# The last level of a block inverse in 32x32 products instead of 64x64 ones, in a transformer kernel on one Trainium2 core

## What is computed

```python
def step(state, inp):
    r_t, w_t, k_t, v_t, kk_t, a_t = inp
    sa = jnp.einsum('bhij,bhj->bhi', state, -kk_t)
    state = (state * w_t[:, :, None, :] + sa[..., None] * (kk_t * a_t)[:, :, None, :]
             + v_t[..., None] * k_t[:, :, None, :])
    return state, jnp.einsum('bhij,bhj->bhi', state, r_t)
```

## Time and profile before

| What | us |
|---|---|
| Median of three runs | 1789.96 |
| Lowest, highest | 1787.77, 1790.02 |
| The profiled execution's own time | 1789.94 |
| Its span in the trace | 1788.6 |
| TensorE busy in the span | 1765.4 |
| VectorE, ScalarE, GpSimd busy | 1155.0, 945.4, 128.3 |

### The profile page before, as it was taken

The page is one execution under the profiler, slowest core; times in us unless marked ns, Lnnn a source line. Parts: engine busy times, 40 slices in busy tenths (PEclk is TensorE's granted clock), DMA queues, the critical chain, the costliest instruction groups (busy, mean ns, idle before and its releaser), DMA issues.

```text
span 1788.6 us, 26360 instructions
## 1 busy us (share of the span) xinstructions
PE 1765.4 (99%) x10762; PEld 1476.6 (83%) x10762; DVE 1155.0 (65%) x1589; ACT 945.4 (53%) x1433; POOL 128.3 (7%) x90
## 2 busy tenths in 40 slices
PE   9999999999999999999999999999999999999999
PEld 6888888888888888888888878888888888888887
DVE  5555678676555565556786755555697557697556
ACT  6454675345544454447653554444646554656553
POOL 0100010141000000000002210000002000002000
PEclk9999999999999999999999999999999999999999
DMA  8755542134555557555421436555554455554564
GB/s 285 279 190 186 173 152 85 61 105 130 187 185 186 186 187 253 186 169 188 142 84 61 140 116 223 189 188 170 165 180 156 166 193 193 174 177 153 174 190 130
DMA packets 84343, 301.12 MB, mean 168 GB/s; under 512 B 9728, under 2 KB 10880, under 8 KB 83712
## 3 DMA queue, kind: packets, MB, share of 16 engines
q1 hardware_dynamic: 80192, 289.44, 49.1%
q10 hardware_dynamic: 3712, 8.56, 1.4%
q0 software_dynamic: 320, 1.45, 0.3%
HBM read 298.36 MB, written 1.05 MB: 167 GB/s over the span
## 4 chain that ended last, share of the span: by engine, by line
PE 88%; DVE 6%; ACT 4%; issue 1%; DMA 1%; POOL 0%; SPq 0%; DVEq 0%; ACTq 0%
PE ps L400 25%; PE ps L402 25%; PE ps L401 25%; DVE wlo L380 1%; ACT whi L339 1%; PE ps L623 1%; PE ps L1278 1%; PE ps L1266 1%; DMA raw<-stream 1%; DVE a_lo L476 1%; PE ps L2680 1%; PE ps L809 1%; PE ps L460 1%; PE ps L423 1%; PE ps L421 1%
## 5 line engine op out<-in xcount | busy, mean ns | idle before, releaser
L380 DVE TENSOR_TENSOR wlo<-raw,whi 128x1024 fp32r<-128x1024 f32 (+1 forms) x545 | 668.9, 1236 | 360.1 <-ACT whi L339 358.6
L339 ACT ACTIVATE whi<-raw 128x1024 fp32r<-128x1024 f32 (+1 forms) x545 | 570.7, 1053 | 454.2 <-PE ps L402 423.7
L400 PE MATMUL ps<-whi,a_hi 128*128 128x512 f32 x1712 | 677.2, 396 | 5.9 <-DVE a_lo L2013 2.0
L402 PE MATMUL ps<-whi,a_lo 128*128 128x512 f32 x1712 | 664.7, 388 | 0.0
L401 PE MATMUL ps<-wlo,a_hi 128*128 128x512 f32 x1712 | 663.7, 388 | 0.0
L400 PEld LDWEIGHTS ps<-whi,a_hi 128*128 128x128 f32 x1712 | 321.5, 188 | 74.5 <-issue 4.7
L402 PEld LDWEIGHTS ps<-whi,a_lo 128*128 128x128 f32 x1712 | 321.3, 188 | 67.6
L401 PEld LDWEIGHTS ps<-wlo,a_hi 128*128 128x128 f32 x1712 | 321.9, 188 | 61.6
L400 PE MATMUL ps<-whi,h_hi 128*128 128x512 f32 x336 | 131.6, 392 | 0.0
L402 PE MATMUL ps<-whi,h_lo 128*128 128x512 f32 x336 | 130.9, 390 | 0.0
L401 PE MATMUL ps<-wlo,h_hi 128*128 128x512 f32 x336 | 130.8, 389 | 0.0
(11 more groups left out here) (330 smaller groups left out, 1680.6 us busy)
## 6 DMA issues: line engine op xcount, KB each, us to landing
raw<-stream SPq DMA_DIRECT2D x545, 512.0 KB, 3.4
arena<-rows ACTq DMA_DIRECT2D x2, 1026.0 KB, 13.8
arena<-mem_turned ACTq DMA_DIRECT2D x2, 1024.0 KB, 9.1
arena<-lora ACTq DMA_DIRECT2D x2, 768.0 KB, 6.6
arena<-x_turned SPq DMA_DIRECT2D x4, 256.0 KB, 6.4
x_res<-x SPq DMA_DIRECT2D x2, 512.0 KB, 9.4
arena<-mem ACTq DMA_DIRECT2D x1, 1024.0 KB, 12.2
arena<-rows ACTq DMA_DIRECT2D x2, 512.0 KB, 4.6
```

Source lines behind the costliest of these rows:

```text
L339: self.split_hi.mark(act.activation(self.weights(self.whi, u), self.weights(self.raw, u), ACT.Copy), u)
L380: self.split_lo.mark(dve.tensor_tensor(self.weights(self.wlo, u), self.weights(self.raw, u), self.weights(self.whi, u).bitcast(F32), ALU.s ...
L400: pe.matmul(out, a_h, hi, start=start, stop=False, skip_group_check=True)
L402: last = pe.matmul(out, a_l, hi, start=False, stop=True, skip_group_check=True)
```

## The change

The last level gets a function of its own, `pe_rw_last_level`, that `pe_mix` calls in place of `pe_rw_level(l, 5)`. It has the same waits, marks and number of products. Each product now loads 32 rows x 32 columns and streams 32 columns: the first half computes only the rows 32 to 63 and columns 0 to 31 of the product in between (rows `down`, columns `first`), from the matrix's rows `up` and columns `last`. The second computes only the block of rows `up` and columns `last`, from the rows `down`. The rest of each bank keeps what was there, which the mask doesn't let through. ScalarE and VectorE are unchanged, and so is the order of all engines.

```diff
@@ pe_rw_level
             for h in range(8):
                 for c in range(2):
                     co = slice(c * HD, (c + 1) * HD)
-                    pair = (T[co, 0, h, :], X[co, h, :]) if lv < 5 else (X[co, h, :], T[co, 0, h, :])
-                    ins = pe.matmul(self.x8(t)[co, h, :], *pair, start=True, stop=True, skip_group_check=True)
+                    ins = pe.matmul(self.x8(t)[co, h, :], T[co, 0, h, :], X[co, h, :], start=True, stop=True,
+                                    skip_group_check=True)
+            m.mark(ins, "level", l, t, lv)
+
+    def pe_rw_last_level(self, l):
+
+        pe, m, lv = self.nc.tensor, self.rw_pe, 5
+        first, last = slice(0, HD // 2), slice(HD // 2, HD)
+        rows = [(slice(c * HD, c * HD + HD // 2), slice(c * HD + HD // 2, (c + 1) * HD)) for c in range(2)]
+        for t in range(NT):
+            pe.wait_ge(*self.rw_dve("T", l, t, lv - 1))
+            for h in range(8):
+                for up, down in rows:
+                    ins = pe.matmul(self.x8(t)[down, h, first], self.MK[up, t, 2 * (h % 4) + h // 4, 0, last],
+                                    self.T2[t][up, 1, h, first], start=True, stop=True, skip_group_check=True)
+            m.mark(ins, "level x", l, t, lv)
+        for t in range(NT):
+            pe.wait_ge(*self.rw_act("X", l, t, lv))
+            pe.wait_ge(*self.rw_dve("turned", l, t, lv - 1))
+            for h in range(8):
+                for up, down in rows:
+                    ins = pe.matmul(self.x8(t)[up, h, last], self.XG[t][down, h, first], self.T2[t][down, 0, h, last],
+                                    start=True, stop=True, skip_group_check=True)
             m.mark(ins, "level", l, t, lv)
@@ pe_mix
         self.pe_rw_gate(l, 0, 2)
-        self.pe_rw_level(l, 5)
+        self.pe_rw_last_level(l)
         pe.wait_ge(*self.rw_act("bonus", l))
         self.pe_rw_gate(l, 1, 3)
```

More of the change, by code:

```diff
@@ L1264, in pe_rw_level @@
                 for c in range(2):
-                    co = slice(c * HD, (c + 1) * HD)
-                    ins = pe.matmul(self.x8(t)[co, h, :], self.MK[co, t, 2 * (h % 4) + h // 4, 0, :], self.T2[t][co, 1, h, :],
-                                    start=True, stop=True, skip_group_check=True)
+                    co, n = slice(c * HD, (c + 1) * HD), 2 * (h % 4) + h // 4
+                    ins = pe.matmul(self.x8(t)[co, h, :], self.MK[co, t, n, 0, :], self.T2[t][co, 1, h, :], start=True,
+                                    stop=True, skip_group_check=True)
             m.mark(ins, "level x", l, t, lv)
```

## The result

| | Runs | Lowest | Median | Highest | Mean granted clock of a run |
|---|---|---|---|---|---|
| Before | 19 | 1786.22 | 1787.77 | 1791.12 | not recorded |
| With the change | 19 | 1787.32 | 1793.07 | 1794.52 | 0.992 to 0.997 |

The change makes the kernel slower: the ratio is 1.0017, 95% interval 1.001 to 1.0024, some 3 us. The medians lie 5.3 us apart: both kernels' runs stand in clusters, and the middle run falls into different ones. The forecast was 1786.6 us with a range from 1783.9 to 1790.1. It was wrong.

A forecast was written before the change was run, and what follows sets the result against it. TensorE, busy for 99% of the span, was taken as the bound. Savings of 1.4 us in layer 1 and 1.9 us in layer 0 made 3.3 us off 1789.94, giving 1786.6 us, range 1783.9 to 1790.1.

The forecast's parts named there:

- What bounds the kernel: Whole kernel: TensorE, busy 99% of the span; time off its row counts unless the next wait gives it back.
- Pace: Last level's products: a pair of records takes 30 ns instead of 58, in proportion to the columns loaded.
- both floors: Last level's record pace: L1214's 27 to 30 ns a record, and the skill's about 25 ns between starts.
- The level at the full clock: Last level in layer 1: 2.5 us in place of 3.9, 1.4 us less, with ScalarE's copies as its bound.
- The lower clock lasts until 339.8, if it lasts as long as before: Last level and gate in layer 0: the low clock ends at the same time as before, giving 1.9 us less.
- The clock falls once more: Rival, behind L1424: a further 6.9 us stretch at half clock costs up to 3.45 us, giving 1790.1; chance 0.12.
- thin products keep the clock low: Rival, last level: 32-column products double layer 0's low stretch and bring two in layer 1, 1797.0 us; chance 0.06.
- The clock falls less often: Rival, last level: no fall in the median execution, 2.5 us in both layers, giving 1784.0 us; chance 0.20.

The follow-up runs named there:

- e6: The kernel before, with its eight two-column products issued four between level 4's halves and four behind it: 1786.53 us, ratio 0.9992.
- e10: e8 with the second gate's first product moved between the halves of the last level: 1783.53 us, ratio 0.9969 to the kernel before.
- e2: The change, but streaming 64 columns instead of 32, still on 32 rows with 32 columns loaded: 1793.27 us, ratio 1.0021 to the kernel before.
- e7: The change, with the eight two-column products issued four and four as in e6: 1790.97 us, ratio 1.0012 to the kernel before.
- e9: The change run once more, with no edit: 1789.47 us, ratio 1.0016 to the kernel before.
- e5: The change, but loading 64 columns instead of 32, still on 32 rows with 32 columns streamed: 1799.23 us, ratio 1.0059 to the kernel before.
- e8: e1 with the eight two-column products issued four and four as in e6: 1783.83 us, ratio 0.9975 to the kernel before.
- e1: The change, but contracting over 64 rows instead of 32, the added rows bringing only zeros: 1784.64 us, ratio 0.9983 to the kernel before.

## Why the prediction was wrong

**What bounds the kernel: right.** In e6 to e10 and in every cluster at clock 1.000 the time follows TensorE's row of work. No wait took the gain back.

**Pace: near, with half of its reason.** I took 30 ns for a pair of records. The 64 records in 1.13 us of e10, whose products also load and stream 32 columns, give 35 ns a pair with start and drain; inside the row the starts come alternately 7 and 25 ns apart, 32 ns a pair. That is below both floors that I had held against it: the 27 to 30 ns a record of L1214 were no bound for products that stream 32 columns. But I had let the time go with the columns loaded. e2 shows that the streamed ones bind as well: 32 loaded and 64 streamed took 1.78 to 1.91 us. The proportion came out because the change halves both.

The Trainium skill, "TensorE: Matmul & The Clock Gate", section "Wait — 56ns, not 53.3ns?", says that starts never come closer than about 25 ns. That is not so here: 1.13 us over 64 records is 17.7 ns on average, for float32 pairs on different rows of the array. The Trainium skill, "TensorEngine Tiling (Array Packing)", section "Instruction Overhead", says that a product of one column takes as long as one of sixty. The trace doesn't bear that out for float32: the own duration of a product was 214 ns with 64 streamed columns (e2) and 191 ns with 32 (the change), both with 32 loaded, and the row of 64 records took 1.78 to 1.91 us against 1.20.

**The level at the full clock: right.** 1.4 us was forecast, 1.36 measured (9.88 against 8.52). The copies became its bound. Over both layers that is 2.7 us: the runs at 1.000 show it, 1783.5 to 1783.9 in e7 against 1786.0 to 1787.1 in e6.

**"The lower clock lasts until 339.8, if it lasts as long as before": wrong.** This is the step of the sum that failed. I let the products change and kept the falls as they were, one of 6.9 us in one layer, and so counted 1.9 us of gain in it. Both its length and the count of one were wrong. These pieces stand behind the gate in the kernel before, in layer 0 with the fall and in layer 1 without, and in the first profile of the change, in layer 0 without and in layer 1 with it:

```profile
348.76 0.61 PE ps L1368 x16
965.86 0.61 PE ps L1368 x16
...
343.92 0.61 PE ps L1389 x16
963.43 0.61 PE ps L1389 x16
```

Counted from the bonus, a layer with a fall took 18.85 us before (348.76 - 329.91) and 18.21 with the change (963.43 - 945.22), 0.6 us less and not 1.9. A layer without one took 15.79 (965.86 - 950.07) and 14.38 (343.92 - 329.54). So a fall costs 3.8 us with 32 rows in use, and lasts 10.2 us, where it cost 3.1 and lasted 6.9. That is 1.3 us of the sum. The larger part is that falls come more often: a second one is another 3.8 us. None of the change's 30 runs was without a fall, and e9's profile has one in each layer. The lowest of the 30 was 1787.32, 3.6 us above 1783.7. One such fall gives 1787.5, two give 1791.4. The cluster at 1789, with a mean clock of 0.996, fits one longer fall (an estimate: 0.004 x 1789 / 0.5 = 14 us at the lower clock), the runs at 1793 to 1794.6, with 0.992 and 0.993, two falls of which one or both are longer; no trace of these clusters was kept, so this is inferred from the clocks. The kernel before has no fall in 30 of the 80 runs with a recorded clock, and its highest run took 1791.70.

**The rivals.** "The clock falls once more" and "thin products keep the clock low" were the right mechanism, the second in its first sentence: products of 32 columns don't bring the clock back. But I gave them 0.12 and 0.06, and dismissed the first because 64-column products had run at 1.00 in this place and the gates stay. The first argument was about the products that the change removes. The second was not borne out: in layer 1 the clock stayed low through the whole gate. The price of the second, 1797.0, lies above every run; the highest took 1794.59. "The clock falls less often" was wrong in sign. "Thin" also named the wrong side: I wrote of columns, and e2 and e5 show that the rows matter.

**The trace had the warning.** One run of three before was 2.2 us faster than the others, and one layer of two had fallen in the profile. Both said that this stretch stood at the edge. A change that makes just this stretch lighter should have been given more than the 0.06 that I gave to ending slower.

## What to carry to other kernels

Where a profile shows a fall of TensorE's clock, or runs in clusters, look at the stretch ahead of it. Here it stood at an edge, and a change that uses less of the array there has to be priced with the clock, not only with its products. A block product can be cut in the columns it loads and streams while it contracts over as many rows as before: with zeros in the added rows that gave here the whole saving of time (35 ns a pair of records against 58) and falls no longer than before. Together with the split bonus there was no fall in 21 runs (e8 and e10). And work that hardly uses the array (here eight products of two columns) was better spread between other products than issued in one piece: that alone took the spread of the kernel before from 5 us to 1.

## What the runs showed of the hardware

- Of two products with the same number of array cells, 64 rows x 32 columns (e1) had falls of the clock down to 0.998 in a run's mean, with a stretch of 3.5 us; 32 rows x 64 columns (e5) had 0.991 to 0.994, with a stretch of 16.8 us.
- Streaming 64 columns instead of 32 on 32 rows (e2) did not help: a mean clock down to 0.991, up to 1800.4 us, though five of twelve runs had no fall.
- Small float32 products on different row groups issued at an average of 17.7 ns a record with 32 columns loaded and streamed (e10; starts alternately 7 and 25 ns apart), 28 to 30 ns with 32 loaded and 64 streamed (e2).
- The clock stayed low through 4.0 us of 512-column products behind the thin level (2.00 us each for L1457 and L1458 in layer 1 of the change, in place of 1.05 each in its layer 0).
- Eight products of 128 loaded and 2 streamed columns, 1.88 us in one piece, came with falls in 14 of 25 runs (a mean clock of 0.997 to 0.999); issued four and four (e6), all 11 runs were at 1.000.
